# A ring of five weight buffer sets for the experts, a gather in two halves, and fourteen products into an unread bank

## The chip, the cores and the metric

The program runs on one core of a Trainium2 chip. The metric is device time in microseconds (us) of that core, lower is better.

## The reference, cut to what matters

The program computes one layer for 256 prompt tokens and 8 sample tokens. The last part, to which the change belongs, is a mixture of 32 experts of which each token uses two:

```python
def hier_moe(h, lw):
    lg = h @ w_router_group + b_router_group          # 4 groups
    g = argmax(softmax(lg))
    le_g = (h @ w_router_expert + b_router_expert)[group g]   # 8 experts in it
    topv, topi = lax.top_k(softmax(le_g), 2)
    comb = one_hot(eid) * (pg_top * topv / sum(topv))  # (tokens, 32)
    out = 0
    for e in range(MOE_EXPERTS):                       # 32
        act = silu(h @ w_exp_gate[e]) * (h @ w_exp_up[e])      # 1024 -> 256
        out = out + comb[:, e:e+1] * (act @ w_exp_down[e])     # 256 -> 1024
    return out
```

`h` is the normed input of the block, 264 rows of 1024. All is float32.

## The kernel before, in words

Each engine runs a program of its own and they meet at semaphores. SP (SyncE) issues the weight loads on one queue, in the order in which they are written. TensorE (PE) multiplies, ScalarE (ACT) and VectorE (DVE) empty PSUM banks.

The experts are taken four at a time: a quad, eight quads in all. Each expert has 32 slots, so the four share the 128 columns of a product. The weights of a quad are three sets of four pieces of 1 MB: gate (`g0` to `g7` in this text), up (`u0` to `u7`) and down (`d0` to `d7`). There is SBUF for five sets. `piece(kind, q, j)` gives their place: two places alternate for gate, two for up, and there is one place for down. So `g2` goes where `g0` was, `u2` where `u0` was, and `d1` where `d0` was. SP waits on `gate_filled`, `up_filled` or `down_filled1`, which say that PE is through with the set that stood there. The order of the loads is g0 u0 d0 g1 u1 (issued while earlier stages run), then g2 u2 d1, g3 u3 d2, and so on to g7 u7 d6, then d7 as eight half pieces: four of the left halves of the columns, then four of the right halves.

Ahead of the experts stands the choice. PE turns the normed tokens (`turn_tokens`, L978 and L982) and computes the router's sums (`route`, L961 and L963). DVE chooses experts in a chain of small operations (L2204 to L2229) and gives `chosen`; PE counts tokens per expert (L1006 to L1016); DVE finds the slots of quad 0 (`find_slots`, L2248); PE gathers the tokens of the quad (`gather`).

`gather(n)` multiplies a 0/1 matrix (`one_r`) by the stored tokens into banks 4 and 5 (L1026 to L1032), multiplies the 0/1 matrix by the tokens' norms into two columns of bank 0 (L1039), and transposes the gathered rows (L1043) once both halves have been copied out. `HG` is then the stationary operand of gate and up. The copies of bank 4 are ACT's, those of bank 5 are DVE's. All of them and ACT's copy `RSLOT` of the norms count on one semaphore, `gathered_stored`, and `gate_up` waits for all five.

PE's order in a step of quad q is: gate and up of q (`gate_up`, L1065), gather of q+1, the transpose of the activation (`turn`, L1073), then `finish` of quad q-1: transposes of the weighted 0/1 matrix (L1096), down (L1079, left half and right half), and `back` (L1088), whose eight products DVE adds into `X1` (L2314). The last step finishes quads 6 and 7, and `X1` goes out as `yT` in three stores.

If more than 32 tokens fall on one expert, another path with more rounds is taken (`rounds > 1`). `by_rounds` reads the largest count and branches; here `rounds` is 1. The path with one round is written as step 0, a loop of three passes over two steps, and step 7.

Of the kernel before, what the change touches and what calls it, by code (L numbers as in the profile page):

```python
# [125 lines left out]
def build_program(nc, ins, outs):  # L126
    ctx = ExitStack()
    with ctx:
# [315 lines left out]
        down_in = sem("down_in")  # L444
# [66 lines left out]
        def _(pe):  # L511
# [488 lines left out]

            pe.wait_ge(sem("chosen"), 1)
# [16 lines left out]
            def gather(n, silus=None):  # L1018
# [32 lines left out]
            def experts(rounds):  # L1051
                moved = 1 if rounds > 1 else 0

                def gate_up(buf, q, n):
                    pe.wait_ge(sem("gathered_stored"), 5 * (n + moved) + 5)
                    for bank, kind in enumerate(("gate", "up")):
# [6 lines left out]
                        for k in range(KT):  # L1063
                            for j in range(QUAD):
                                mm = pe.matmul(psum[bank][SLOTS * j:SLOTS * (j + 1), 0:D_FF],  # L1065
                                               HG[:, k, SLOTS * j:SLOTS * (j + 1)], piece(kind, buf, j)[:, k, :],
                                               start=(k == 0), stop=(k == KT - 1))
                        mm.then_inc(sem(f"{kind}_filled"), 1)
# [7 lines left out]
                def down(half, buf, which):  # L1076
                    for f in range(FF_T):
                        for j in range(QUAD):
                            mm = pe.matmul(psum[2 + half][SLOTS * j:SLOTS * (j + 1), :],  # L1079
                                           ACTT[which][:, f, SLOTS * j:SLOTS * (j + 1)],  # L1080
                                           piece("down", buf, j)[:, FF_T * half + f, :], start=(f == 0), stop=(f == 1))
                    mm.then_inc(sem(f"down_filled{half}"), 1)

# [7 lines left out]
                def finish(buf, q, n):  # L1091
# [7 lines left out]
                    pe.wait_ge(down_in, q * (16 * QUAD) + 16 * QUAD)  # L1099
                    pe.wait_ge(sem("actT_ready"), n + 1)  # L1100
                    down(0, buf, which)
                    if is_last(q):
                        pe.wait_ge(sem("back_ready"), n + 1)
                        back(0, n)
                        pe.wait_ge(sem("last_half_in"), 16 * QUAD)
                        down(1, buf, which)
                    else:
                        down(1, buf, which)
# [4 lines left out]
                def step(buf, q):  # L1113
                    gate_up(buf, q, q)
                    if not is_last(q):
                        gather(q + 1, q + 1)
# [12 lines left out]
                if rounds > 1:  # L1129
                    pe.wait_ge(sem("gathered_stored"), 5)  # L1130
# [6 lines left out]
        def _(sp):  # L1137
# [69 lines left out]
            def load_piece(kind, e, q, j):  # L1207
                src = ins[f"w_exp_{kind}"][e].rearrange("p (k f) -> p k f", f=512 if kind == "down" else D_FF)
                sp.dma_start(piece(kind, q, j), src).then_inc(  # L1209
                    {"gate": gate_in[q % 2], "up": up_in[q % 2], "down": down_in}[kind], 16)  # L1210
# [48 lines left out]
            def experts(rounds):  # L1259

                def next_pieces(kind, q, buf):
                    if kind == "down":
                        sp.wait_ge(sem("down_filled1"), q * rounds)
                    else:
                        sp.wait_ge(sem(f"{kind}_filled"), (q - 1) * rounds)
# [3 lines left out]
                with sp.Fori(0, QUADS // 2 - 1) as it:  # L1269
                    for b in range(2):  # L1270
# [1225 lines left out]
```

## Time and profile before

| what | value |
|---|---|
| three runs | 885.2, 885.23, 887.98 us, median 885.23 us |
| profiled execution, own time | 886.53 us |
| its span, first to last instruction | 884.7 us |
| PE busy | 794.8 us, 90% of the span |
| DVE busy | 505.2 us, 57% |
| ACT busy | 314.0 us, 35% |
| DMA moved | 231.92 MB, mean 262 GB/s |

The profiled execution took 1.83 us more than its span, and 1.3 us more than the median. The share of busy time is a mean over stages with different limits; the experts' stage starts near 659 us of the span. Times in the rows are counted from the span's start. PEclk is TensorE's granted clock, where 1.00 is 2.4 GHz and 0.50 is 1.2 GHz.

### The profile page before, as it was taken

What the parts mean: (1) busy time and instruction counts of PE and PEld (TensorE: products, weight loads), DVE (VectorE), ACT (ScalarE), POOL (GpSimd) and SP (SyncE); (2) the same over time, 40 slices, a digit from 0 to 9 for tenths busy, and PEclk for the clock granted to TensorE, in tenths of its full rate; (3) what the DMA queues carried; (4) which work ended last, traced back from release to release, by engine and by line L of the source; (5) the groups of instructions that cost most, each with busy time, mean ns of one, the idle gap of its engine ahead of it and who ended that gap; (6) DMA issues with size and microseconds to landing.
All of it is one profiled execution on the core that took longest, in us unless ns stands there. A gap on an engine that the chain in (4) does not pass through costs nothing.

```text
span 884.7 us, 14773 instructions
## 1 busy us (share of the span) xinstructions
PE 794.8 (90%) x6020; PEld 639.5 (72%) x6020; DVE 505.2 (57%) x915; ACT 314.0 (35%) x618; POOL 37.3 (4%) x50
## 2 busy tenths in 40 slices
PE   4899999999899998899998899999979977877865
PEld 4899999899777786578865799998945534443422
DVE  4463889584789539797868557576441323212312
ACT  4444545354343343544663745343321101000100
POOL 0000000000101001012111000000000000000000
PEclk9999999999999999899999999999959999888977
DMA  9335455365526347798899595856848899999965
GB/s 374 120 112 229 154 182 189 116 246 185 191 96 226 131 169 269 239 315 284 291 351 390 159 358 193 312 185 229 324 209 337 331 422 423 422 422 422 420 254 206
DMA packets 36397, 231.92 MB, mean 262 GB/s; under 512 B 3920, under 2 KB 4200, under 8 KB 12384
## 3 DMA queue, kind: packets, MB, share of 16 engines
q1 hardware_dynamic: 28512, 199.56, 58.1%
q0 software_dynamic: 7824, 31.51, 11.0%
q8 instruction: 43, 0.70, 0.3%
q14 instruction: 18, 0.15, 0.1%
HBM read 216.72 MB, written 15.37 MB: 262 GB/s over the span
## 4 chain that ended last, share of the span: by engine, by line
PE 61%; DVE 15%; DMA 14%; SPq 4%; ACT 3%; issue 2%; POOL 0%; DVEq 0%; ACTq 0%; POOLq 0%
PE bank L553 15%; PE bank L925 13%; PE bank L541 8%; DMA M<-in_w_exp_up 6%; PE bank L1065 4%; SPq L1209 4%; DMA M<-in_w_exp_down 3%; PE bank L1079 3%; PE bank L592 3%; PE bank L562 2%; DVE at_r L235 2%; PE bank L1026 2%; DMA W<-in_w_in 1%; DVE M L1903 1%; PE bank L625 1%
## 5 line engine op out<-in xcount | busy, mean ns | idle before, releaser
L235 DVE TENSOR_TENSOR at_r<-W,at_r 128x1024 fp32r<-128x1024 f32 x100 | 121.2, 1222 | 96.8 <-ACT at_r L1406 64.1
L541 PE MATMUL bank<-HN,W 128*128 128x264 f32 x640 | 156.2, 399 | 2.6 <-DMA W<-in_w_in 2.6
L541 PEld LDWEIGHTS bank<-HN,W 128*128 128x128 f32 x640 | 124.0, 196 | 28.8 <-issue 3.6
L553 PE MATMUL bank<-at_r,at_r 128*128 128x264 f32 (+1 forms) x1152 | 141.5, 284 | 2.2 <-DVE M L1742 2.2
L553 PEld LDWEIGHTS bank<-at_r,at_r 128*128 128x128 f32 x1152 | 140.1, 188 | 3.0 <-DVE at_r L235 2.4
L925 PE MATMUL bank<-at_r,at_r 128*128 128x264 f32 x960 | 120.7, 287 | 5.2 <-DVE at_r L235 5.2
L925 PEld LDWEIGHTS bank<-at_r,at_r 128*128 128x128 f32 x960 | 119.1, 191 | 5.9 <-DVE at_r L235 5.8
L1382 ACT ACTIVATE M<-bank 128x264 f32<-128x264 f32 (+4 forms) x110 | 43.2, 407 | 165.0 <-PE bank L541 85.6
L1065 PE MATMUL bank<-M,W 128*32 128x256 f32 x1024 | 71.1, 442 | 31.4 <-DMA M<-in_w_exp_up 28.6
L1065 PEld LDWEIGHTS bank<-M,W 128*32 128x32 f32 x1024 | 36.3, 127 | 65.2 <-DMA M<-in_w_exp_up 31.1
L1406 ACT ACTIVATE at_r<-W 128x1024 fp32r<-128x1024 f32 x60 | 62.4, 1053 | 17.3 <-PE bank L553 13.2
L1492 ACT ACTIVATE at_r<-W 128x1024 fp32r<-128x1024 f32 x40 | 41.5, 1054 | 50.8 <-DMA W<-in_w_br_ssm 25.4
L2290 DVE SCALAR_TENSOR_TENSOR M<-bank,M 128x256 f32<-128x256 f32 x8 | 3.9, 484 | 94.4 <-PE bank L1065 94.4
L1088 PE MATMUL bank<-M,W 128*128 128x264 f32 x128 | 38.6, 428 | 3.3 <-DVE W L2305 0.8
L1088 PEld LDWEIGHTS bank<-M,W 128*128 128x128 f32 x128 | 20.7, 196 | 25.6 <-DVE HN L2314 11.8
L1558 ACT ACTIVATE M<-M 128x128 f32<-128x128 f32 x128 | 38.2, 392 | 2.8 <-DMA M<-in_state_ssm 2.8
L2314 DVE TENSOR_TENSOR HN<-HN,bank 128x264 f32<-128x264 f32 x64 | 27.4, 429 | 17.0 <-PE bank L1088 16.5
L1079 PE MATMUL bank<-M 128*32 128x512 f32 x256 | 32.1, 642 | 5.0 <-DMA M<-in_w_exp_down 5.0
L1783 DVE SCALAR_TENSOR_TENSOR M<-M 128x255 f32<-128x255 f32 (+2 forms) x72 | 29.8, 475 | 0.0
L1673 ACT ACTIVATE W<-bank 128x512 f32<-128x512 f32 x8 | 4.8, 597 | 68.6 <-PE bank L1029 68.6
L1684 ACT ACTIVATE M<-bank,M 128x256 f32<-128x256 f32 x8 | 3.8, 473 | 68.4 <-PE bank L1065 68.4
L2000 DVE TENSOR_TENSOR M<-M 128x2048 f32<-128x2048 f32 x8 | 18.3, 2293 | 14.5 <-ACT M L1558 14.4
(355 smaller groups left out, 987.7 us busy)
## 6 DMA issues: line engine op xcount, KB each, us to landing
W<-in_w_in SPq DMA_DIRECT2D x42, 1024.0 KB, 5.0
M<-in_w_exp_gate SPq DMA_DIRECT2D x32, 1024.0 KB, 21.1
M<-in_w_exp_up SPq DMA_DIRECT2D x32, 1024.0 KB, 26.0
M<-in_w_exp_down SPq DMA_DIRECT2D x28, 1024.0 KB, 18.0
W<-in_w_mem_kv SPq DMA_DIRECT2D x8, 1024.0 KB, 7.1
M<-in_mem_kT SPq DMA_DIRECT2D x8, 1024.0 KB, 6.2
M<-in_state_ssm POOLq DMA_DIRECT2D x8, 1024.0 KB, 9.1
out_s_ssm<-M POOLq DMA_DIRECT2D x8, 1024.0 KB, 7.2
```

The lines of the kernel that those rows point to most:

```text
L235: return eng.tensor_tensor(low, x, high.bitcast(F32), ALU.subtract)
L541: mm = pe.matmul(bank[:, 0:n], w[:, k, P * c:P * (c + 1)], x[:, k, 0:n], start=(k == 0), stop=(k == KT - 1))
L553: mm = pe.matmul(bank[:, 0:n], w[:, k, :], x_[:, k, 0:n], start=(k + i == 0), stop=(k == KT - 1 and i == 2))
L925: mm = pe.matmul(bank[:, 0:T], w[:, k, :], x_[:, k, :], start=(first and k + i == 0), stop=(last and k == KT - 1 and i == 2))
L1065: mm = pe.matmul(psum[bank][SLOTS * j:SLOTS * (j + 1), 0:D_FF], HG[:, k, SLOTS * j:SLOTS * (j + 1)], piece(kind, buf, j)[:, k, :], start=( ...
L1079: mm = pe.matmul(psum[2 + half][SLOTS * j:SLOTS * (j + 1), :], ACTT[which][:, f, SLOTS * j:SLOTS * (j + 1)], piece("down", buf, j)[:, FF_T ...
L1088: pe.matmul(psum[6 + m % 2][:, 0:T], DOWNED[:, P * m:P * (m + 1)], BACK, start=True, stop=True).then_inc(sem("tile_filled"), 1)
L1209: sp.dma_start(piece(kind, q, j), src).then_inc({"gate": gate_in[q % 2], "up": up_in[q % 2], "down": down_in}[kind], 16)
L1382: drains(a.activation(dst, b[0:rows, 0:n] if src is None else src(b), ACT.Copy), name)
L1406: a.activation(like_raw(w_split(name, c)[0], name), raw_half(name, c), ACT.Copy).then_inc(sem(f"high_ready{c}"), 1)
L1492: a.activation(branch_high(h), branch_raw(h), ACT.Copy).then_inc(sem("branch_rounded"), 1)
L1558: last = a.activation(h, h, ACT.Copy, scale=EX[:, 1, j, b_:b_ + 1])
```

## The change

Four things are changed; parts that only rename semaphores are left out below.

1. For one round the five sets form a ring: each load goes to the set that is used earliest, so d1 goes where g1 was, g3 where u1 was, u3 where d0 was, d2 where g2 was. `piece(..., ring=True)` gives the place. d7 goes where u6 was. Its right halves count on two semaphores, by pairs of pieces, and `last_down` takes the pairs one after the other.
2. For one round the loop is gone: the eight steps are written out on every engine.
3. The gather is worked in halves. Each half of the transposes waits only for the copy of its own bank, and gate's products on the second half of `HG` wait for that half alone. The norms' products move behind gate's products of the same quad; ACT copies `RSLOT` just before its SiLU; DVE's `find_slots` of the next quad waits for the norms' products, since these read the 0/1 matrix.
4. While the experts are chosen PE makes fourteen products of 512 columns, `ident_r` by stored tokens, into bank 1. DVE copies one column of them to a place that nobody reads, behind its operation `D4`, and the count's products wait for that copy, as they use the same bank.

```diff
-        def piece(kind, q, j):
-
-            o = {"gate": (free1, free4)[q % 2], "up": (free2, free5)[q % 2], "down": free3}[kind][j]
+        ring_sets = [free1, free2, free3, free4, free5]
+        ring_loads = [("gate", 0), ("up", 0), ("down", 0), ("gate", 1), ("up", 1)]
+        ring_uses = [("gate", 0), ("up", 0)]
+        for q in range(2, QUADS + 1):
+            if q < QUADS:
+                ring_loads += [("gate", q), ("up", q)]
+            ring_loads.append(("down", q - 1))
+            ring_uses += [("gate", q - 1), ("up", q - 1), ("down", q - 2)]
+        ring_home = {load: ring_sets[n] for n, load in enumerate(ring_loads[:5])}
+        for used, load in zip(ring_uses, ring_loads[5:]):
+            ring_home[load] = ring_home[used]
...
             if rounds == 1:
-                step(0, 0)
-                with eng.Fori(0, QUADS // 2 - 1) as it:
-                    step(1, it * 2 + 1)
-                    step(0, it * 2 + 2)
-                step(1, QUADS - 1)
+                for q in range(QUADS):
+                    step(q % 2, q)
...
+            b = opened("unread", 1)
+            for part in range(2):
+                wait_drained(pe, ("htok", ("high", part), 0))
+            for i in range(14):
+                mm = pe.matmul(b[:, :], ident_r[:, :], token_rows(0, i % 2, 0), start=True, stop=True)
+            full(mm, "unread")
             pe.wait_ge(sem("chosen"), 1)
...
-                if silus is None:
-                    pe.wait_ge(drained[0], uses[0])
-                else:
-                    pe.wait_ge(sem("silu"), silus)
-                for t, rows in enumerate((P, P, BATCH_S)):
-                    pe.matmul(psum[0][:, 256:258], ONE[0:rows, t].rearrange("p j s -> p (j s)"),
-                              RTOK[0:rows, t:t + 2], start=(t == 0), stop=(t == 2))
-                pe.wait_ge(sem("gathered_stored"), 5 * n + 2)
-                for k in range(KT):
-                    mm = pe.transpose(psum[4 + k // 4][:, P * (k % 4):P * (k % 4 + 1)], DOWNED[:, P * k:P * (k + 1)], ident)
-                    if k % 4 == 3:
-                        mm.then_inc(sem(f"gathered{k // 4}"), 1)
+                for half, per_quad in enumerate((2, 2)):
+                    pe.wait_ge(sem(f"gathered_stored{half}"), per_quad * n + 1)
+                    for k in range(4):
+                        mm = pe.transpose(psum[4 + half][:, P * k:P * (k + 1)],
+                                          DOWNED[:, 512 * half + P * k:512 * half + P * (k + 1)], ident)
+                    mm.then_inc(sem(f"gathered{half}"), 1)
...
                 def gate_up(buf, q, n):
-                    pe.wait_ge(sem("gathered_stored"), 5 * (n + moved) + 5)
...
                         for k in range(KT):
+                            if kind == "gate" and k % 4 == 0:
+                                pe.wait_ge(sem(f"gathered_stored{k // 4}"), 2 * (n + moved) + 2)
...
+                        if kind == "gate":
+                            for t, rows in enumerate((P, P, BATCH_S)):
+                                mm = pe.matmul(psum[0][:, 256:258], ONE[0:rows, t].rearrange("p j s -> p (j s)"),
+                                               RTOK[0:rows, t:t + 2], start=(t == 0), stop=(t == 2))
+                            mm.then_inc(sem("norm_up_filled"), 1)
...
+                def last_down(buf, q, which):
+                    for arrived, count, pieces in ((gate_in[0], 32, (0, 1)), (up_in[0], 32, (2, 3))):
+                        pe.wait_ge(arrived, landed_all + count)
+                        for f in range(FF_T):
+                            for j in pieces:
+                                mm = pe.matmul(psum[3][SLOTS * j:SLOTS * (j + 1), :],
+                                               ACTT[which][:, f, SLOTS * j:SLOTS * (j + 1)],
+                                               held("down", buf, q, j)[:, FF_T + f, :], start=(f == 0), stop=(f == 1))
+                    mm.then_inc(sem("down_filled1"), 1)
...
+                if rounds == 1:
+                    for used, (kind, q) in zip(ring_uses, ring_loads[5:-1]):
+                        set_used(*used)
+                        for j in range(QUAD):
+                            load_piece(kind, q * QUAD + j, q, j, piece(kind, q, j, True))
+                    set_used(*ring_uses[len(ring_loads) - 6])
+                    set_used("down", QUADS - 3)
...
                 def gate_silu(n, which):
-                    act.wait_ge(sem("gate_filled"), n + 1)
+                    act.wait_ge(sem("norm_up_filled"), 2 * n + 1)
+                    a.activation(RSLOT[which], psum[0][:, 256:257], ACT.Copy).then_inc(sem("silu"), 1)
+                    act.wait_ge(sem("silu"), 2 * n + 1)
                     a.activation(SG, psum[0][:, 0:D_FF], ACT.Silu, scale=RSLOT[which]).then_inc(sem("silu"), 1)
...
+            b = wait_filled(dve, "unread")
+            drains(v.tensor_copy(at("S", 232, 233), b[:, 0:1]), "unread")
             b = wait_filled(dve, "twice")
...
                         dve.wait_ge(sem("slots_ready"), q + 1)
+                        dve.wait_ge(sem("norm_up_filled"), 2 * q + 1)
                         find_slots(q + 1, q + 1)
```

The first place is on PE, from the gather of quad 0 to the first products of gate. Before, the norms' products stand between gather and transposes, and the eight transposes have one wait:

```order
1288 L1032 MATMUL bank<-at_256_r,at_384_r 128x256
1289 L1039 MATMUL bank<-M,at_384_r 128x2 [waits drained0]
1290 L1039 MATMUL bank<-M,at_384_r 128x2 x2
1291 L1043 MATMUL bank<-M,W 128x128 [waits gathered_stored]
1292 L1043 MATMUL bank<-M,W 128x128 x7
1293 L449 TENSOR_LOAD worst [waits worst_ready]
1294 L451 COMPARE_AND_BRANCH
1295 L1065 MATMUL bank<-M,W 32x256 [waits gate_in0,gathered_stored]
1296 L1065 MATMUL bank<-M,W 32x256 x31
```

The same place on PE of the change:

```order
1290 L1049 MATMUL bank<-at_256_r,at_384_r 128x256
1291 L1054 MATMUL bank<-M,W 128x128 [waits gathered_stored0]
1292 L1054 MATMUL bank<-M,W 128x128 x3
1293 L1054 MATMUL bank<-M,W 128x128 [waits gathered_stored1]
1294 L1054 MATMUL bank<-M,W 128x128 x3
1295 L463 TENSOR_LOAD worst [waits worst_ready]
1296 L465 COMPARE_AND_BRANCH
1297 L1080 MATMUL bank<-M,W 32x256 [waits gathered_stored0,gate_in0,drained0]
1298 L1080 MATMUL bank<-M,W 32x256 x15
1299 L1080 MATMUL bank<-M,W 32x256 [waits gathered_stored1]
1300 L1080 MATMUL bank<-M,W 32x256 x15
1301 L1086 MATMUL bank<-M,at_384_r 128x2 x3
```

The norms' products went behind gate's 32, and transposes and gate's products wait for one half each.

The second place is on SP, the loads from g2 to d1. In the loop before, each load at an address that changes has an instruction ahead of it, and d1 waits for down of quad 0:

```order
90 L1209 DMA M<-in_w_exp_up 128x2048 [waits up_filled]
91 L1209 DMA M<-in_w_exp_up 128x2048 x3
92 L1209 ISA [waits down_filled1]
93 L1209 DMA M<-in_w_exp_down 128x2048
94 L1209 ISA
95 L1209 DMA M<-in_w_exp_down 128x2048
```

In the change, where each row with a wait is the first piece of a set (g2, u2, d1, g3, u3):

```order
80 L1240 DMA M<-in_w_exp_gate 128x2048 [waits gate_filled]
81 L1240 DMA M<-in_w_exp_gate 128x2048 x3
82 L1240 DMA M<-in_w_exp_up 128x2048 [waits norm_up_filled]
83 L1240 DMA M<-in_w_exp_up 128x2048 x3
84 L1240 DMA M<-in_w_exp_down 128x2048 [waits gate_filled]
85 L1240 DMA M<-in_w_exp_down 128x2048 x3
86 L1240 DMA M<-in_w_exp_gate 128x2048 [waits norm_up_filled]
87 L1240 DMA M<-in_w_exp_gate 128x2048 x3
88 L1240 DMA M<-in_w_exp_up 128x2048 [waits down_filled1]
```

d1 now waits for gate of quad 1, and it is u3 that waits for down of quad 0.

The third place is on PE, between the last token product and the count's first product. Of the change:

```order
1273 L1016 MATMUL bank<-at_6144_r,at_128_r 128x512 [waits drained4,drained3,drained1]
1274 L1016 MATMUL bank<-at_6144_r,at_128_r 128x512 x13
1275 L1023 MATMUL bank<-at_96_r,at_80_r 40x32 [waits drained1,drained0,tables_rounded,chosen]
1276 L1024 MATMUL bank<-at_96_r,at_128_r 128x32
1277 L1025 MATMUL bank<-at_96_r,at_128_r 128x32
```

The fourteen products are new; before, nothing stood there, and the count's first product waited as well for `chosen`.

## Rows read from the trace of the kernel before

**Rows 1.** Windows: stretches, busy times, PEclk, DMA share and GB/s.
```profile
687.00:693.00 6.00, 5.92 (x42) 2.34 (x41) 3.26 (x8) 0.60 (x1) 0.00 (x0) 1.00 0.25 82
693.00:851.00 158.00, 126.06 (x1172) 66.63 (x1171) 40.69 (x88) 12.11 (x26) 0.00 (x0) 0.90 1.01 422
```

**Rows 2.** Chain that ended last, in order of time: start, length, what.
```profile
829.94 23.76 DMA M<-in_w_exp_down
```

**Rows 3.** Timeline of SP's queue: start, length, line, what, count.
```profile
690.99 2.08 SPq L1209 DMA_DIRECT2D M<-in_w_exp_down  x4
...
859.14 4.64 SPq L1280 DMA_DIRECT2D M<-in_w_exp_down  x8
```

**Rows 4.** Timelines of DVE, then ACT, from the choice to the first SiLU.
```profile
647.00 0.17 DVE L2231 TENSOR_TENSOR M<-M 128x12 f32<-128x12 f32 x1
...
648.43 0.22 DVE L2238 TENSOR_TENSOR M<-bank,at_r 128x64 f32<-128x64 f32 x1 [0.94 <-PE bank L1012]
...
655.21 0.69 DVE L2261 COPY W<-bank 128x512 f32<-128x512 f32 x1 [2.64 <-PE bank L1032]
...
658.39 1.28 ACT L1684 ACT_TABLE_LOAD   x1
665.27 0.47 ACT L1684 ACTIVATE M<-bank,M 128x256 f32<-128x256 f32 x1 [5.60 <-PE bank L1065]
```

**Rows 5.** Windows of TensorE's clock, columns as in rows 1.
```profile
642.10:643.30 1.20, 0.00 (x0) 0.00 (x0) 0.99 (x7) 1.20 (x4) 0.00 (x0) 1.00 1.05 437
643.40:663.80 20.40, 15.50 (x79) 10.18 (x83) 9.02 (x38) 3.91 (x9) 0.00 (x0) 0.50 0.44 186
...
748.10:752.50 4.40, 0.00 (x0) 0.00 (x0) 0.00 (x0) 0.47 (x1) 0.00 (x0) 1.00 1.01 421
```

**Rows 6.** Timeline of PE, 647 to 663 us, idle time and releaser behind.
```profile
647.02 0.24 PE L1006 MATMUL bank<-at_r,at_r 8*40 8x32 f32 x1 [4.93 <-DVE at_r L2229]
...
649.68 2.04 PE L1026 MATMUL bank<-at_r,at_r 128*128 128x512 f32 x4 [0.49 <-DVE at_r L2248]
...
655.10 1.53 PE L1039 MATMUL bank<-M,at_r 128*128 128x2 f32 x6
656.56 1.97 PE L1043 MATMUL bank<-M,W 128*128 128x128 f32 x8
659.31 3.22 PE L1065 MATMUL bank<-M,W 128*32 128x256 f32 x28 [0.78 <-DVE W L2263]
```

**Rows 7.** Timeline of PE, 668 to 691 us, the same products for later quads.
```profile
668.58 1.20 PE L1026 MATMUL bank<-at_r,at_r 128*128 128x512 f32 x4
...
671.70 0.92 PE L1039 MATMUL bank<-M,at_r 128*128 128x2 f32 x6
672.56 1.09 PE L1043 MATMUL bank<-M,W 128*128 128x128 f32 x8
...
674.52 7.11 PE L1065 MATMUL bank<-M,W 128*32 128x256 f32 x128 [0.65 <-DVE W L2263]
...
687.15 3.64 PE L1079 MATMUL bank<-M 128*32 128x512 f32 x32
```

**Rows 8.** Timeline of PE at the end.
```profile
861.57 2.36 PE L1088 MATMUL bank<-M,W 128*128 128x264 f32 x8 [0.17 <-DVE HN L2314]
864.46 0.60 PE L1096 MATMUL bank<-M 128*128 128x128 f32 x3 [0.52 <-DVE HN L2314]
867.41 2.45 PE L1079 MATMUL bank<-M 128*32 128x512 f32 x16 [2.36 <-DMA M<-in_w_exp_down]
870.60 3.87 PE L1088 MATMUL bank<-M,W 128*128 128x264 f32 x8 [0.74 <-issue]
874.40 2.44 PE L1079 MATMUL bank<-M 128*32 128x512 f32 x16
```

**Rows 9.** The page: its first line, and the queue of instructions (packets, MB, share).
```profile
span 884.7 us, 14773 instructions
...
q8 instruction: 43, 0.70, 0.3%
```

More of the change, by code:

```diff
@@ L302, in build_program, with piece @@
         assert y_end + 6 * PIECE <= MAP["Z"][0]
-        def piece(kind, q, j):
-            o = {"gate": (free1, free4)[q % 2], "up": (free2, free5)[q % 2], "down": free3}[kind][j]
+        ring_sets = [free1, free2, free3, free4, free5]
[9 more added lines that the diff above has]
+            ring_home[load] = ring_home[used]
+        def piece(kind, q, j, ring=False):
+            o = (ring_home[kind, q] if ring else
+                 {"gate": (free1, free4)[q % 2], "up": (free2, free5)[q % 2], "down": free3}[kind])[j]
             return M[:, o:o + PIECE].rearrange("p (k n) -> p k n", n=512 if kind == "down" else D_FF)
@@ L443, in build_program @@
         up_in = [sem(f"up_in{b}") for b in range(2)]
-        down_in = sem("down_in")
+        down_in = [sem(f"down_in{b}") for b in range(2)]
+        landed_all = 16 * QUAD * (QUADS // 2)
         def by_rounds(eng, experts):
@@ L1074, in turn, with down @@
                     mm.then_inc(sem("act_turned"), 1)
-                def down(half, buf, which):
+                def down(half, buf, q, which):
                     for f in range(FF_T):
@@ L1104, in finish @@
                         back(0, n)
-                        pe.wait_ge(sem("last_half_in"), 16 * QUAD)
-                        down(1, buf, which)
+                        last_down(buf, q, which)
                     else:
-                        down(1, buf, which)
+                        down(1, buf, q, which)
                         pe.wait_ge(sem("back_ready"), n + 1)
@@ L1115, in step @@
                     if not is_last(q):
-                        gather(q + 1, q + 1)
+                        gather(q + 1)
                     turn(q)
@@ L1129, in experts @@
                 if rounds > 1:
-                    pe.wait_ge(sem("gathered_stored"), 5)
+                    for half in range(2):
+                        pe.wait_ge(sem(f"gathered_stored{half}"), 2)
+                pe.wait_ge(drained[0], uses[0])
                 steps(pe, rounds, step, alone)
@@ L1264, in next_pieces, with set_used @@
                     else:
-                        sp.wait_ge(sem(f"{kind}_filled"), (q - 1) * rounds)
+                        name, per_quad = {"gate": ("gate_filled", 1), "up": ("norm_up_filled", 2)}[kind]
+                        sp.wait_ge(sem(name), (q - 1) * (rounds * per_quad))
                     for j in range(QUAD):
                         load_piece(kind, q * QUAD + j, buf, j)
-                with sp.Fori(0, QUADS // 2 - 1) as it:
-                    for b in range(2):
-                        q = it * 2 + b + 2
-                        next_pieces("gate", q, b)
-                        next_pieces("up", q, b)
-                        next_pieces("down", q - 1, 1 - b)
-                sp.wait_ge(sem("down_filled1"), (QUADS - 1) * rounds)
+                def set_used(kind, q):
+                    name, per_quad = {"gate": ("gate_filled", 1), "up": ("norm_up_filled", 2), "down": ("down_filled1", 1)}[kind]
+                    sp.wait_ge(sem(name), per_quad * (q + 1))
+                if rounds == 1:
[5 more added lines that the diff above has]
+                    set_used("down", QUADS - 3)
+                else:
+                    with sp.Fori(0, QUADS // 2 - 1) as it:
+                        for b in range(2):
+                            q = it * 2 + b + 2
+                            next_pieces("gate", q, b)
+                            next_pieces("up", q, b)
+                            next_pieces("down", q - 1, 1 - b)
+                    sp.wait_ge(sem("down_filled1"), (QUADS - 1) * rounds)
                 for half in range(2):
@@ L1699, in alone @@
                 def alone(buf, q, n):
-                    store_gathered(n + 1, 0)
+                    store_gathered(n + 1)
                     gate_silu(n, 0)
@@ L2230, in _ @@
                                       T24.unsqueeze(2).to_broadcast(shape), ALU.mult), "chosen")
-            done(dve, v.tensor_tensor(D4, LG[:, :, 0:GROUPS], over(MXG, GROUPS), ALU.subtract), "route_args")
+            done(dve, v.tensor_tensor(D4, LG[:, :, 0:GROUPS], over(MXG, GROUPS), ALU.subtract), "chosen")
             dve.sem_inc(sem("tile_added"), 2)
+            b = wait_filled(dve, "unread")
+            drains(v.tensor_copy(at("S", 232, 233), b[:, 0:1]), "unread")
             b = wait_filled(dve, "twice")
```

46 lines of the change are left out of this document (24 added, 22 removed).

## The prediction

> **What bounds the kernel now.** I read the windows of the experts' stage first. From 693 to 851 us the DMA engines are busy all the time at 422 GB/s while PE works 126 of 158 us [rows 1]. So this stretch is set by the weights: a set of four pieces is 4.19 MB, and at 422 GB/s it takes 9.94 us. What PE, DVE or ACT do in it costs nothing as long as each set comes free in time. Three things outside that stretch then set the end: when the first set comes free, where the queue runs dry, and what is left to do when the last weights are in.
>
> The queue runs dry twice. From 687 to 693 us it moves 82 GB/s instead of 422, which is a hole of 6 x (1 - 82/422) = 4.8 us. It ends with SP's issue of d1 at 690.99 us [rows 3], and PE's down products of quad 0 end at 687.15 + 3.64 = 690.79 us [rows 7]: d1 waits for the one down set. The second place is the end: the chain has d6 landing at 829.94 + 23.76 = 853.70 us [rows 2], and d7 is issued only at 859.14 us [rows 3], again behind the down products that read the same set.
>
> The first set, g0's, comes free when gate of quad 0 is through. ACT's SiLU starts at 665.27 us behind it [rows 4], so I put that at 665.2 us. The way there is a pure chain with no load on it: `chosen`, PE's count from 647.02 us, gather from 649.68 us, norms, transposes, a copy, gate from 659.31 us [rows 6]. And nearly all of it runs at half clock: PEclk is 0.50 from 643.4 to 663.8 us, after PE did nothing from 642.1 us on [rows 5]. The same products a quad later, at full clock, show what that costs [rows 7].
>
> **The ring.** The hole first. In the ring d1 waits for gate of quad 1. That is done at 674.52 + 7.11/2 = 678.1 us [rows 7], 12.9 us after the first release. The queue has g2 and u2 to move by then, 19.9 us of it, so d1 is queued about 7 us early. The next that is late is looked for: g3 waits for up of quad 1 (681.6 us, 16.4 after the release; the queue has 29.8 us), u3 for down of quad 0 (25.6 after; the queue has 39.8 us). From there on each load waits for the use of the set five places ahead, with four sets of 9.94 us between, while PE has finished within some 5 us of a landing. Nothing is late. Gain: the whole hole, 4.8 us.
>
> The end next. d7 goes to u6's place and can stand in the queue behind d6. Its left halves land 5.0 us after d6, its right halves 9.9 us after. PE's work between d6's landing and the last down is down and back of quad 6 and the transposes, which end at 864.46 + 0.60 = 865.06 us [rows 8], 11.4 us after d6. So the weights are there before PE wants them, and PE sets the end. It saves its wait (867.41 - 865.06 = 2.35 us). It also comes to the last products without a pause. The two down halves (2.45 and 2.44 us) and the back between them (3.87 us) [rows 8] ran partly at half clock; at full clock a half of down is 3.64/2 = 1.82 us [rows 7] and a back of four tiles 2.36 us [rows 8]. That is 0.63 + 0.62 + 1.51 = 2.76 us. Sum 5.1 us; 2.35 if the clock falls there as before. Splitting the last down by pairs of pieces then gains nothing, since all has landed.
>
> **The chain to the first release, without the clock.** The copy of the unread bank puts two small DVE operations of some 0.17 us [rows 4] ahead of the count: with the semaphores +0.4 us, so the count starts at 647.4 us. That is the added wait; behind it stand the count and the whole chain. From the end of the gather to gate took 659.31 - 655.10 = 4.2 us [rows 6]. Now it is the copy of bank 5 (0.69 us [rows 4]), half of the transposes (half of 1.97 or of 1.09 us [rows 6, 7]), and 0.2 us of semaphores: 1.9 us at half clock, 1.4 us at full. The read of the largest count by PE had 0.78 us of waiting as its cover [rows 6]; that cover is gone, for which I add 0.2 us (0 to 0.7). ACT now loads its table (1.28 us [rows 4]) between the norms and the first SiLU; up of quad 0 takes 3.55 us meanwhile, which hides it.
>
> **The clock.** The fourteen products have the gather's form, 4 in 1.20 us at full clock or 2.04 at half. From 642.1 us they last 14 x 0.28 = 3.9 us, to 646.0. They end before `chosen`, so they delay nothing if they run at full clock. Then PE has nothing until 647.4 us, ten small products to about 648.2 us, and nothing until the gather at about 649.5 us. The row of before says that a stretch like that is dangerous: the clock fell 1.3 us after the last of a run of small products, though at another place it was still at 1.00 after 4.4 us of nothing [rows 5]. So I work out both.
>
> Clock falls again near the gather's start: count about 1.0 us in place of 1.41, DVE's 1.25 us as now (648.43 to 649.68 [rows 4, 6]), gather from about 649.5 us and nearly all at half clock, 4.9 us, to 654.4; 1.9 + 0.2 us, hence gate from 656.4 us; gate as now 665.2 - 659.31 = 5.9 us: released at 662.3 us. Gain 2.9 us.
>
> Clock stays at full: gather 671.70 - 668.58 = 3.1 us [rows 7], to 652.6; 1.4 + 0.2 us; gate 3.55 us: released at 657.8 us. Gain 7.4 us.
>
> **Sum.** 4.8 + 5.1 + 2.9 = 12.8 us with the clock falling again, 17.3 us with the clock kept. The profiled execution (span 884.7 us, 886.53 with what lies around it) stands 1.3 us above the median. I take the gains from the median: 885.23 - 12.8 = 872.4 us, and 867.9 us. The span should be about 1 us below these.
>
> **The loop written out** I cost at nothing. All code of before came in 43 packets of 0.70 MB [rows 9], under 2 us of the queue's rate even if doubled, and PE has 8.8 us to spare in each quad (worked out below). The Trainium skill, Runtime: NRT & Kernel Launch, section Instruction fetch mechanics, says that a taken branch to code outside the fetched blocks stalls and that straight code is fetched ahead; no run here shows a stall of this kind, and since PE waits for weights there, the rule would move nothing.
>
> **The rivals.** *Clock kept* (above), 867.9 us. For it: 4.4 us of nothing left the clock at 1.00. Against: the fall at 643.4 us.
>
> *The products don't hold the clock at all.* The gather's products are 5.4 us of the same form, and with norms and transposes PE was busy for 15.5 of the 20.4 us at 0.50, and the clock did not rise before gate's products had run [rows 5, 6]. If these products count as little, the clock falls at 643.4 us as before; 4.6 of them are done then, and 9.4 at 0.51 us last to 648.2 us. The count starts 1.2 us later than before, and the release comes at 650.9 + 5.4 + 1.9 + 0.2 + 5.9 = 664.3 us, gain 0.9 us: 885.23 - 10.8 = 874.4 us. The Trainium skill, TensorE: Matmul & The Clock Gate, Part 4, says that transposes do not count as the engine's activity in the same way; the fourteen have an identity as an operand but are plain products, so by the page they would count, and by the gather's rows it is open.
>
> *The ring leaves a wait that I don't see*, the hole or the end as before: 877 us.
>
> *No change*: both the ring's gains and the chain's fail. Nothing in the rows speaks for it.
>
> *Slower*: the written-out code comes late. A packet is 16 KB; 14773 instructions in 0.70 MB [rows 9] are 47 bytes each, and a step's some 206 products with their weight loads then need about one and a quarter packets (an estimate), which travel on engines that are full at 422 GB/s. A quad takes PE 21.0 us (from 674.52 us to 690.79, and two backs of 2.36 us [rows 7, 8]) and the queue 29.8 us, so the slack is 8.8 us and it decides from about 7 us a packet. At 12 us a packet it would be 6 us a quad and 37 us over six quads: 909 us. Against it: PE's program was straight up to the end of quad 0 before as well, and PE waits for nothing of the kind there.
>
> **How the numbers follow.** Clock falls again 0.47; clock kept 0.28; products don't hold it 0.14; a wait left in the ring 0.05; no change 0.03; slower 0.03. The likeliest gives 872.4 us. The range goes down to the kept clock with 1.4 us for a chain that is shorter than I think, 866.5 us, and up to the products that hold nothing and an end at half clock in part, 876.0 us. A difference under 0.3%, 2.7 us, can't be told from none. Faster 0.94, same 0.03, slower 0.03.
>
> **What would show it.** The DMA share near 1.0 with no hole from the first release to the last weights, about 189 us; SP issuing d1 right behind gate of quad 1 and d7 ahead of d6's landing; PE without a wait for a load between back of quad 6 and the last back; gate of quad 0 starting near 656.4 us (or 654.2) with PEclk at 0.50 (or 1.00). I am wrong if the queue runs dry somewhere, if the fourteen products end later than `chosen`, or if PE stands idle in quads where the weights have landed.

## The result, and the profile after

The changed kernel took 876.36 us (median of 4 runs, 875.45 to 877.39) beside 885.22 us for the kernel before (4 runs): a ratio of 0.9893, 95% interval 0.9871 to 0.9916. In a second comparison it took 874.12 us beside 886.63 us: a ratio of 0.9861, interval 0.9834 to 0.9887. So it is faster: by the medians 8.9 us in the first and 12.5 us in the second comparison, by the ratios 9.5 and 12.3 us. The forecast was 12.8 us.

The times of one kernel spread by several us from run to run (before: 882.09 to 889.24 us in 23 runs of one comparison). So the span is read here in stretches between marks that every profile has: R, where DVE first reads the router's sums; T, where SP issues g2; A, where PE starts down of quad 6, when d6 has landed; and the end of the span.

| profile | R | R to T | T to A | A to end | span |
|---|---|---|---|---|---|
| before | 641.64 | 23.79 | 188.31 | 30.96 | 884.7 |
| changed | 643.90 | 20.49 | 184.16 | 25.85 | 874.4 |
| changed, again | 639.81 | 19.26 | 184.26 | 25.47 | 868.8 |

All three stretches of the forecast are shorter: by 3.3 or 4.5, by 4.1 and by 5.1 or 5.5 us. R, which lies ahead of everything that was changed, stood 2.3 us later in the first profile of the changed kernel and 1.8 us earlier in the second. For the first pair that is 3.30 + 4.15 + 5.11 - 2.26 = 10.3 us, the difference of the spans.

The windows of the changed kernel (columns as in [rows 1]) show the queue of the weights. The hole of 6 us at 82 GB/s is gone, and where before stood still behind d6, d7 follows:

```profile
686.00:692.00 6.00, 5.92 (x45) 2.48 (x44) 3.30 (x7) 0.60 (x1) 0.00 (x0) 1.00 1.00 415
692.00:848.00 156.00, 127.65 (x1180) 67.11 (x1179) 41.89 (x89) 12.87 (x27) 0.00 (x0) 0.90 1.01 420
850.00:858.00 8.00, 7.68 (x44) 3.26 (x36) 3.25 (x8) 0.60 (x1) 0.00 (x0) 0.92 0.80 320
```

SP's queue in the changed kernel, against [rows 3]: the first row is g2, the third d1, now 12.8 us behind g2 and not 25.6, and d7 (L1325) has been handed over by 844.5 us, ahead of d6's landing at 848.5 us.

```profile
664.39 2.26 SPq L1240 DMA_DIRECT2D M<-in_w_exp_gate  x4
668.84 1.77 SPq L1240 DMA_DIRECT2D M<-in_w_exp_up  x4
677.19 2.59 SPq L1240 DMA_DIRECT2D M<-in_w_exp_down  x4
...
824.69 19.77 SPq L1325 DMA_DIRECT2D M<-in_w_exp_down  x8
```

PE at the end of the changed kernel, against [rows 8]. Between the transposes (L1126) and down of quad 7 (L1099) there is no wait for a load any more, and back and both halves of down run at full clock (2.36, 1.92 and 1.94 us in place of 3.87, 2.45 and 2.44). The first row is down of quad 6, which begins at mark A:

```profile
848.55 4.94 PE L1099 MATMUL bank<-M 128*32 128x512 f32 x32 [1.95 <-DMA M<-in_w_exp_down]
...
858.86 0.59 PE L1126 MATMUL bank<-M 128*128 128x128 f32 x3 [0.52 <-DVE HN L2362]
859.39 1.92 PE L1099 MATMUL bank<-M 128*32 128x512 f32 x16
862.08 2.36 PE L1118 MATMUL bank<-M,W 128*128 128x264 f32 x8 [0.77 <-issue]
864.37 1.94 PE L1109 MATMUL bank<-M 128*32 128x512 f32 x16
```

PE ahead of the first release in the changed kernel, against [rows 6]. The fourteen products (L1016) took 5.64 us and ended 1.5 us behind the choice, which was at 649.24 us; the gather (L1043) still ran at half clock; gate of quad 0 (L1080) ran at full clock, 3.66 us:

```profile
644.14 1.05 PE L989 MATMUL bank<-at_r,at_r 128*128 128x128 f32 x4
645.00 0.31 PE L993 MATMUL bank<-at_r,at_r 128*40 128x128 f32 x1
645.10 5.64 PE L1016 MATMUL bank<-at_r,at_r 128*128 128x512 f32 x14
651.19 0.18 PE L1023 MATMUL bank<-at_r,at_r 8*40 8x32 f32 x1 [0.45 <-DVE M L2281]
...
653.37 2.04 PE L1043 MATMUL bank<-at_r,at_r 128*128 128x512 f32 x4 [0.82 <-DVE at_r L2296]
...
658.79 1.70 PE L1054 MATMUL bank<-M,W 128*128 128x128 f32 x8
660.68 3.66 PE L1080 MATMUL bank<-M,W 128*32 128x256 f32 x64 [0.19 <-ACT W L1720]
```

The clock in the same profile, in windows chosen at its steps. It had fallen at 642.9 us, while PE was still on the router's last small products, with the last turns to come, and before the first of the fourteen. During the fourteen it rose, and it fell again at the gather:

```profile
642.90:649.60 6.70, 6.70 (x25) 5.73 (x25) 5.00 (x27) 3.11 (x10) 0.00 (x0) 0.51 1.00 419
649.80:653.00 3.20, 2.30 (x14) 1.57 (x13) 1.17 (x6) 0.13 (x1) 0.00 (x0) 0.99 1.03 433
653.20:659.90 6.70, 6.53 (x16) 4.08 (x17) 3.34 (x15) 0.60 (x1) 0.00 (x0) 0.50 0.20 86
660.00:664.40 4.40, 4.21 (x69) 2.77 (x68) 0.69 (x1) 0.54 (x1) 0.00 (x0) 0.99 0.02 6
```

### The profile page after: what moved, and what is told of

Its sections match the earlier page's. It is cut to its first block, busy times and chain, and to the rows that moved or that the text cites. A ratio compares the mean times of both kernels' runs of the same rounds, so it can differ in the third digit from the quotient of the medians.

```text
span 874.4 us, 14498 instructions
## 1 busy us (share of the span) xinstructions
PE 796.0 (91%) x6034; PEld 641.3 (73%) x6034; DVE 505.3 (58%) x916; ACT 315.5 (36%) x618; POOL 37.4 (4%) x50
## 4 chain that ended last, share of the span: by engine, by line
PE 57%; DVE 15%; SPq 14%; DMA 8%; ACT 3%; issue 2%; POOL 0%; DVEq 0%; ACTq 0%; POOLq 0%
PE bank L564 15%; SPq L1240 14%; PE bank L936 13%; PE bank L552 9%; DMA M<-in_w_exp_down 3%; PE bank L603 3%; PE bank L573 2%; PE bank L1080 2%; DVE at_r L235 2%; DMA W<-in_w_in 2%; DVE M L1949 1%; PE bank L1099 1%; PE bank L636 1%; DMA out_p_ssm<-M 1%; PE bank L1043 1%
## 5 line engine op out<-in xcount | busy, mean ns | idle before, releaser
L1080 PE MATMUL bank<-M,W 128*32 128x256 f32 x1024 | 68.6, 428 | 23.6 <-DMA M<-in_w_exp_up 22.5
L1080 PEld LDWEIGHTS bank<-M,W 128*32 128x32 f32 x1024 | 35.0, 123 | 52.6 <-DMA M<-in_w_exp_up 22.9
L1118 PE MATMUL bank<-M,W 128*128 128x264 f32 x128 | 36.8, 410 | 4.0 <-DVE HN L2362 1.2
L1099 PE MATMUL bank<-M 128*32 128x512 f32 x240 | 28.7, 619 | 1.9 <-DMA M<-in_w_exp_down 1.9
## 6 DMA issues: line engine op xcount, KB each, us to landing
M<-in_w_exp_gate SPq DMA_DIRECT2D x32, 1024.0 KB, 25.5
```

The source lines that it names most:

```text
L1118: pe.matmul(psum[6 + m % 2][:, 0:T], DOWNED[:, P * m:P * (m + 1)], BACK, start=True, stop=True).then_inc(sem("tile_filled"), 1)
```

## The experiments

Theory A, after the first comparison: the ring gives nearly all of the gain, and the products buy about what they cost. Its rival B: products and halves are worth the 2.9 us that the forecast gave them and something else took 4 us away. All kernels are compared with the kernel before on the same chip; ratios are given with their 95% interval. What the first four runs were to say:

**Without the products** (`e1_no_products`). The changed kernel without these lines, the opening of the bank and its waits ahead of them (cut here), and DVE's copy:

```diff
-            for i in range(14):
-                mm = pe.matmul(b[:, :], ident_r[:, :], token_rows(0, i % 2, 0), start=True, stop=True)
-            full(mm, "unread")
```

> The changed kernel without the fourteen products and without the copy that reads them. Theory A (in the changed kernel the clock had fallen at 642.9 us, before the first product at 645.1 us, so they ran for 5.6 us instead of 3.9, ended 1.5 us after the choice and bought back about as much as they cost): within 1.5 us of the changed kernel, 875 to 877.5 us, rather below it. Theory B (the products are worth the 2.9 us that the forecast gave to the clock and the halves, and something else took 4 us away): 878.5 us or more.

Measured: 872.09 us, ratio 0.9861 (0.9826 to 0.9895). The median lies below the range of either theory. Part of that is not the products' doing, as far as one profile can say: its A to end is 23.5 us where the changed kernel has 25.5 to 25.9, and 1.3 us of the difference is down of quad 6, which ran at full clock here (3.64 us, where the changed kernel has 4.94). The change doesn't touch these products, and over the kernels with the ring they took 3.64 to 6.10 us.

```profile
846.27 3.64 PE L1093 MATMUL bank<-M 128*32 128x512 f32 x32 [2.31 <-DMA M<-in_w_exp_down]
```

**The products alone** (`e2_products_alone`). The kernel before with the same lines and the copy added.

> The kernel before with the fourteen products and the copy as its only change. Theory A: 884.5 to 887 us, no gain. Theory B: 881 to 883.5 us. With either, the release of the first set moves by as much as the total, since the queue of the weights is full behind it.

Measured: 887.07 us beside 886.28, ratio 1.0008 (0.9985 to 1.0031): no gain.

**Old places** (`e3_old_places`). The changed kernel, but

```diff
-        for used, load in zip(ring_uses, ring_loads[5:]):
-            ring_home[load] = ring_home[used]
+        ring_uses = [(kind, q - 1 if kind == "down" else q - 2) for kind, q in ring_loads[5:]]
```

and each load at its place of before.

> The changed kernel with the sets at their old places and the old waits (g2 behind g0, u2 behind u0, d1 behind d0, d7 behind d6); products, halves and the written-out loop stay. Theory A (the ring is all of the gain): 884 to 886 us, with the hole of some 5 us and the late d7 back. Theory B (ring worth 6 us, the rest 3): 882 to 883 us.

Measured: 885.49 us, ratio 0.9987 (0.9965 to 1.0008). The first release came 4.7 us earlier behind R than in the kernel before (R to T 19.1 us in place of 23.8), but T to A was 1.9 us longer, 190.2 in place of 188.3 (1.2 us of that is in the profile of the steps written out alone, below). The hole is back; the window of this kernel there:

```profile
683.00:689.00 6.00, 5.91 (x45) 2.62 (x45) 2.89 (x7) 1.12 (x2) 0.00 (x0) 1.00 0.15 42
```

**The ring alone** (`e4_ring_alone`). The kernel before with the steps written out, `piece(..., ring=True)` and SP's order of waits as in the change.

> The kernel before with the loop written out and the ring of five sets as its only change; gather in one piece, no products. Theory A: the hole (4.8 us) and the end (5.1 us) are gained, 875 to 877 us, as fast as the changed kernel. Theory B: 878.5 to 880 us.

Measured: 875.78 us, ratio 0.9880 (0.9849 to 0.9910), 10.6 us of 886.28.

These four say where the gain is: the ring alone (with the steps written out) has 10.6 us, and all else without the ring 1.2 us, with an interval from 3.1 us faster to 0.7 us slower. B is out for the ring's part; for the 2.9 us of products and halves this interval is too wide to decide. And by the medians the kernel without the products was 14 us faster than before, where the changed kernel had been 9 us faster in a comparison of its own (12.3 and 9.5 us by the ratios). So the changed kernel was compared again, beside its variants.

**The changed kernel again** (`e9_changed_again`), no edit.

> The changed kernel as it is, on the same chip and against the same runs of before as the next three. It took 876.4 us where the kernel without the products took 872.1 us beside other runs. Theory A' (the products cost, by ending after the choice and by their copy): again about 4 us above 872, 875.5 to 877.5 us. Theory J (the difference is the spread from run to run of what lies ahead of the experts, which moved by up to 5 us between the profiles): 872 to 875 us.

Measured: 874.12 us, ratio 0.9861 (0.9834 to 0.9887): the same ratio as without the products. That is in J's range. The interval, 871.9 to 876.6 us, reaches into the range of A' as well, so the whole times exclude a cost of 1 or 2 us no more than a gain of that size.

**d7 late** (`e6_late_d7`).

```diff
-                    set_used("down", QUADS - 3)
+                    set_used("down", QUADS - 2)
```

> The changed kernel with d7 issued only when down of quad 6 is through, its place still in the ring. The forecast's term for the end: 5.1 us more than the changed kernel as run beside it, 5 to 6 us if the clock falls in the pause. If the end is not limited as I think (PE anyway sets it): 0 to 2 us more.

Measured: 878.86 us, ratio 0.9914 (0.9887 to 0.9941), 4.7 us above the changed kernel beside it. The interval of each is some 2.5 us to either side. Its profile has the wait back, and the clock falls in it. From A to the end it took 31.9 us, where the changed kernel has 25.5 to 25.9:

```profile
860.57 3.64 PE L1099 MATMUL bank<-M 128*32 128x512 f32 x16 [3.04 <-DMA M<-in_w_exp_down]
864.97 3.87 PE L1118 MATMUL bank<-M,W 128*128 128x264 f32 x8 [0.76 <-issue]
868.77 2.47 PE L1109 MATMUL bank<-M 128*32 128x512 f32 x16
```

**d1 late** (`e7_late_d1`).

```diff
                         set_used(*used)
+                        if (kind, q) == ("down", 1):
+                            set_used("down", 0)
```

> The changed kernel with d1 issued only when down of quad 0 is through, its place still in the ring. The forecast's term for the hole: 4.8 us more than the changed kernel as run beside it. If the queue would catch up elsewhere: under 2 us more.

Measured: 880.65 us, ratio 0.9923 (0.9897 to 0.9950), 6.5 us by the medians and 5.5 by the ratios above the changed kernel. SP's queue shows d1 26.0 us behind g2, and T to A is 190.4 us in place of 184.2:

```profile
664.54 2.08 SPq L1240 DMA_DIRECT2D M<-in_w_exp_gate  x4
668.98 1.78 SPq L1240 DMA_DIRECT2D M<-in_w_exp_up  x4
690.55 2.11 SPq L1240 DMA_DIRECT2D M<-in_w_exp_down  x4
```

The pause is deeper than in the kernel before. These are 20 us each from 20 us behind T on, of the kernel before, of d1 late and of the changed kernel. Against 419 GB/s the pause costs 20 x (1 - 320/419) = 4.7 us in the first and 20 x (1 - 293/419) = 6.0 us in the second:

```profile
685.40:705.40 20.00, 19.78 (x201) 10.71 (x201) 6.90 (x16) 2.33 (x5) 0.00 (x0) 1.00 0.78 320
684.50:704.50 20.00, 19.49 (x202) 10.59 (x202) 7.61 (x16) 1.84 (x4) 0.00 (x0) 1.00 0.73 293
684.40:704.40 20.00, 19.49 (x202) 10.58 (x201) 7.61 (x16) 1.85 (x4) 0.00 (x0) 1.00 1.01 419
```

**Written out** (`e5_written_out`). The kernel before with

```diff
-                step(0, 0)
-                with eng.Fori(0, QUADS // 2 - 1) as it:
-                    step(1, it * 2 + 1)
-                    step(0, it * 2 + 2)
-                step(1, QUADS - 1)
+                for q in range(QUADS):
+                    step(q % 2, q)
```

> The kernel before with the loop written out and nothing else. The forecast costs it at nothing: within 1 us of before. The windows of the kernels with the loop written out move 419 to 421 GB/s where before moved 422, which over 180 us would be up to 1 us; if fetching code is what takes it, this kernel shows 0.5 to 1 us more than before. If stalls for code held PE up it would be 3 us or more.

Measured: 887.87 us beside 886.63, ratio 1.0016 (0.9996 to 1.0036). The interval, from 0.4 us faster to 3.2 us slower, holds both no difference and the 1 us; 3 us is at its edge. T to A is 189.5 us in place of 188.3, with 421 GB/s from 700 to 850 us where before moved 422. Whether the written-out code costs that 1 us stays open.

The last four ask what the number and the place of the products do. R to T is the mark for it, since it leaves out what happens ahead.

**Six products** (`e8_six_products`): `range(6)` for `range(14)`.

> The changed kernel with six products instead of fourteen. From the profiles so far: from DVE's first read of the router's sums to SP's issue of g2 it takes 23.8 us in before, 21.1 without products, 19.3 to 20.5 with fourteen. If it is the full clock for gate that the fourteen buy (and they pay with 0.7 to 1.9 us on the way to the count), six end too early to buy it: about 21.1 to 21.5 us for that way, total within 1 us of the kernel without products. If any products do: 19.3 us.

Measured: 876.06 us, ratio 0.9886 (0.9866 to 0.9907). R to T 19.8 us, and gate ran at full clock. The expectation of 21.1 to 21.5 us missed. In this profile the clock fell at 648.8 us, at the choice and 3.3 us ahead of the gather, and was back at full 0.3 us ahead of gate:

```profile
648.90:659.00 10.10, 9.04 (x28) 6.35 (x29) 4.73 (x21) 1.34 (x4) 0.00 (x0) 0.50 0.51 216
```

**Spread** (`e10_spread`). The cut parts let DVE signal `halfway` and put the wait for bank 1 behind the three products.

```diff
-            for i in range(14):
+            for i in range(13):
+                if i == 7:
+                    pe.wait_ge(sem("halfway"), 1)
...
+            for i in range(3):
+                pe.matmul(psum[6][:, :], ident_r[:, :], token_rows(0, i % 2, 0), start=True, stop=True)
             gather(0)
```

> The changed kernel with its products spread: seven at once, six when DVE is two thirds through the choice, and three more (bank 6) between the count and the gather, where PE stands idle for 0.8 us. In the changed kernel the clock fell again at the gather's start, and the gather ran 5.4 us instead of 3.1. If spreading holds the clock through the gather, the way from the first read of the router's sums to g2's issue is 16.9 to 17.5 us and the total some 2 us under the changed kernel; if not, 19.3 to 20 us and no gain.

Measured: 872.59 us, ratio 0.9848 (0.9827 to 0.9870), R to T 19.2 us. The lowest ratio of all, but its interval lies over those of the changed kernel and of the one without products.

**The gap filled** (`e11_gap_filled`): the fourteen as they are, and the three ahead of the gather.

> The changed kernel with three more products (bank 6) between the count and the gather, the fourteen as they are. If the pause just ahead of the gather is what lets the clock fall: 17 to 17.5 us from the router's sums to g2's issue. If the pause of 2.4 us ahead of the count is, the clock still falls and the way is 19.3 to 20.5 us.

Measured: 873.46 us, ratio 0.9861 (0.9831 to 0.9891), R to T 19.3 us. The clock was at 1.00 up to the gather and fell there all the same; windows of this kernel before, in and behind the gather:

```profile
642.10:649.90 7.80, 5.45 (x29) 4.09 (x27) 5.83 (x30) 2.77 (x8) 0.00 (x0) 1.00 1.00 420
650.20:656.60 6.40, 6.40 (x17) 3.91 (x18) 3.08 (x13) 0.60 (x1) 0.00 (x0) 0.50 0.36 151
657.40:661.00 3.60, 3.60 (x65) 2.37 (x65) 0.50 (x1) 0.00 (x0) 0.00 (x0) 1.00 0.03 7
```

**24 products** (`e12_24_products`): `range(24)`.

> The changed kernel with 24 products instead of fourteen. At full clock they last 24 x 0.248 = 6.0 us and end about 1 us behind the choice: the count starts 1.7 us late instead of 0.76, so the way is 20.3 us if the clock falls again, or 18 us if it holds through the gather. At half clock they would last up to 9.6 us and put the count 4 us late.

Measured: 875.24 us, ratio 0.9871 (0.9841 to 0.9900). They took 5.80 us; the count started 1.2 us behind the choice, not 1.7, R to T 20.9 us, the gather at half clock.

The marks of all of these, from their profiles. "Choice to count" is the time from `chosen` to PE's first product of the count, "gate" PE's start of gate of quad 0. From R to `chosen` it is 5.3 to 5.4 us in all of them. In the spread and the gap-filled kernel the three added products start 1.29 us behind the count's start:

| profile | choice to count | count to gather | gather to gate | gate to T | R to T | T to A | A to end |
|---|---|---|---|---|---|---|---|
| before | 0.05 | 2.66 | 9.63 | 6.12 | 23.79 | 188.31 | 30.96 |
| written out | 0.05 | 2.66 | 9.63 | 6.27 | 23.96 | 189.52 | 30.68 |
| products alone | 0.75 | 2.18 | 9.64 | 5.84 | 23.77 | 188.45 | 30.87 |
| ring alone | 0.05 | 2.66 | 9.64 | 5.72 | 23.40 | 185.28 | 25.59 |
| without products | 0.05 | 2.66 | 7.33 | 5.74 | 21.12 | 184.17 | 23.53 |
| changed | 1.95 | 2.18 | 7.31 | 3.71 | 20.49 | 184.16 | 25.85 |
| changed, again | 0.76 | 2.17 | 7.26 | 3.71 | 19.26 | 184.26 | 25.47 |
| six products | 0.76 | 2.63 | 7.31 | 3.72 | 19.77 | 185.51 | 26.96 |
| 24 products | 1.20 | 2.18 | 7.32 | 4.87 | 20.93 | 184.00 | 25.54 |
| spread | 0.76 | 2.18 | 7.23 | 3.71 | 19.21 | 184.37 | 25.11 |
| gap filled | 0.75 | 2.18 | 7.32 | 3.71 | 19.33 | 184.12 | 25.42 |
| old places | 0.76 | 2.18 | 6.70 | 4.13 | 19.14 | 190.17 | 31.09 |
| d7 late | 0.77 | 2.18 | 7.28 | 3.71 | 19.31 | 184.10 | 31.89 |
| d1 late | 1.91 | 2.17 | 7.32 | 3.72 | 20.47 | 190.41 | 25.55 |

## Why the prediction was right, and where it was not

**The hole.** Forecast 4.8 us by d1 being queued early. The pause was worth 4.7 us in the kernel before (the 320 GB/s above). T to A fell by 4.1 us, and putting d1 back behind down of quad 0 alone brought 6.2 us back in that stretch, where the pause is 6.0 us. That T to A fell by less may be the written-out code, whose profile has 189.5 us there with the pause still in it, not 188.3; one profile each doesn't show it. The step held. (T to A is 5.3 us more than its 18 sets at 9.94 us, and the last weights were in near 858 us, 194 us behind T where the prediction had about 189. The kernel before has 4.7 us of the same beside its pause, so the gain stands.) The rest of it, that the next late set would be none, held too: cut into stretches of 4 to 10 us, none from 686 to 848 us is under 415 GB/s.

**The end.** Forecast 5.1 us: 2.35 us of waiting and 2.76 us of products at half clock. A to end fell by 5.1 us, and with d7 late again it is 6.0 us longer. Held, the split too: the wait is gone, and back and the halves of down now take 2.36, 1.92 and 1.94 us, 2.5 us less than before (forecast 2.76). Another 0.4 us is down of quad 6, 4.94 us in place of 5.34, which no part of the change explains. Taking the last down by pairs gained nothing, as forecast: 1.94 us, against 1.92 in the ring alone, which does not have it.

**The halves of the gather.** The forecast had 1.9 us (and 0.2) from the gather's end to gate instead of 4.2. From the gather's start to gate it is 7.3 us with the halves and 9.6 without them, 2.3 us shorter. Held in the stretch. R to T without the products is 21.1 us, 2.7 us shorter than before; the last 0.4 us of these lie between gate's start and T, and are there in the ring alone too. No run takes the halves alone away from the changed kernel: the nearest pair, without products against the ring alone, has ratios of 0.9861 and 0.9880 with intervals that overlap, so in the whole times the halves are not shown. PE's read of the count, for which I had added 0.2 us, is hidden: in the changed kernel PE stood for 0.19 us between transposes and gate, and it was ACT's copy that it waited for. The gather itself was sized too low, 4.9 us: it took 5.4 us at half clock, as in the kernel before.

**The products and the clock.** Here the time came out and the way did not: costs and gains that I had not seen set each other off, which is luck. Forecast: the copy costs 0.4 us on the way to the count, the clock falls again near the gather, the gather and gate run at half clock, 2.9 us gained with the halves in it. Measured where the clock still stood at full: choice to count +0.7 us, count to gather -0.5, so the gather began 0.2 us later than in before (the forecast had 649.5 us where its own terms, 647.4 + 1.0 + 1.25, give 649.65, no change). The fall came within 0.7 us of the gather's start as forecast, in all nine profiles with the halves and the products but that of six products. But gate then ran at full clock again, 3.71 us from its start to T in place of 5.74: in all nine but two it was 3.7 us (4.13 with old places, 4.87 with 24 products). That is 2.0 us that I had not given to the case "falls again". And a cost that I had not seen: the clock can have fallen before the first of the fourteen. I had taken for granted that they start at full clock, since before the fall came at 643.4 us, after the turns. In the changed kernel's first profile and in that of d1 late it came during the turns; the fourteen took 5.6 us, ended later than `chosen`, which the prediction gave as a sign of being wrong, and the count started 1.9 us behind the choice. At full clock they took 3.47 us (the forecast had 3.9). Net, the products are worth 0.6 to 1.9 us of R to T beside the kernel without them, and in the times that can't be told from nothing: both ratios are 0.9861, each to some 3 us. In before, without the halves, they are worth nothing by either measure (23.77 to 23.79 us; ratio 1.0008); there the clock, at full up to the gather, was at half up to 668 us, past the start of gate at 664.04. Why gate is at full clock with products and halves and not with either alone was not found; in the spread and the gap-filled kernel three products right ahead of the gather did not change it.

**Why the first comparison showed less.** 8.9 us stood against a forecast of 12.8, and just above my range. By the ratio it is 9.5 us or 875.8 us, just inside. R is the reason for the profile's part. It spread from 639.8 to 646.1 us over the fourteen profiles, by code that is the same in all. For the two profiles of the changed kernel the rows show where most of it arises. The same sixteen products, which follow a load, started 1.3 us later in the first, and took 6.83 us where the second took 3.83:

```profile
479.89 6.83 PE L552 MATMUL bank<-HN,W 128*128 128x264 f32 x16 [2.87 <-DMA W<-in_w_in]
```

```profile
478.57 3.83 PE L552 MATMUL bank<-HN,W 128*128 128x264 f32 x16 [2.66 <-DMA W<-in_w_in]
```

PEclk was 0.51 from 479.1 to 485.8 us in the first and 1.00 over the sixteen in the second. Behind them the two are 4.1 us apart, as at R (643.9 and 639.8 us). In d1 late the clock fell there too, and its R is 644.1 us. So a fall of the clock far ahead of the experts, in code that the change doesn't touch, makes 2.8 of these 4.1 us. For the other profiles it is argued from this one place, not shown. What I left out of the forecast was this spread: with four runs a side the median itself can be off by 2 to 3 us, and the range's upper end should have had it.

**The rivals.** "Clock kept" did not occur: the first gather ran at half clock in every profile, but for the first of its products in the kernel with old places (1.42 us for its first four, where the others have some 2.0). "The products don't hold the clock" has part of the truth: they raised it when it had fallen (the window from 649.8 us above), but did not hold it through the gather. "A wait left in the ring" did not occur. "Slower by late code" is out: written out alone costs 1.2 us by the medians and may cost nothing.

No version was found that is surely faster than the changed kernel. The spread one has the lowest ratio, 0.9848 against 0.9861, which these runs can't tell apart.

## What to carry to other kernels

When a stage is bound by the weights' queue, count three things: when the first buffer comes free, each pause of the queue, and what is left behind the last byte. Giving each load the buffer that is used up first, whatever its kind, removed a pause of 4 to 6 us and 5 us at the end at no cost in space. Compare stretches between marks inside the profile as well as whole times: here the part ahead of the change moved by 4.1 us between two profiles of one and the same kernel, a third of the gain.

## What the runs showed of the hardware

The products of the first gather, 512 columns by a matrix of zeros and ones, ran at half clock, all or (with old places) nearly all of them, also when PEclk was 1.00 and three products of the same form ran right ahead of them (the windows of the gap-filled kernel). So it is not these products by themselves: those of a later quad took 1.20 us for four, at full clock [rows 7]. Right behind the first gather gate's products, small ones on 32 columns of the array, ran at 1.00 in the kernels with products and halves (in two of nine only from 0.8 and 2.4 us behind gate's start on), and at 0.50 for most of gate in the kernels with one or neither.

SP stands at the queue: once it is full, handing over four pieces takes as long as moving them. In the changed kernel four issues take 1.8 to 5.0 us for the first six sets and 8.6 to 12.3 us for each of the twelve from 703.8 us on, about the 9.9 us of a set. From there SP is always busy with loads, and a wait written behind them is reached late:

```profile
804.75 8.66 SPq L1240 DMA_DIRECT2D M<-in_w_exp_up  x4
813.45 11.13 SPq L1240 DMA_DIRECT2D M<-in_w_exp_down  x4
```

The clock's fall is not tied to the same instruction from run to run: in before at 643.4 us, 1.3 us after the last of the turns; in the changed kernel once at 642.9 us, with PE still at work, once not until 648.3 us, at the gather.
